# Activation sums of a seven-product MLP formed in the preceding output blocks, with changed waits and loads around them

## What is computed

```python
def sq_relu_mlp(h, w1, w2):
    u = jax.nn.relu(h @ w1)
    return (u * u) @ w2

x = x + mix                                             # mix = o @ w_out
x = x + sq_relu_mlp(rms_norm(x, norm_mlp[i]), mlp_w1[i], mlp_w2[i])   # 1024 -> 4096 -> 1024
```

## Time and profile before

| | us |
|---|---|
| median of 3 runs | 2312.28 (2311.3 to 2315.58) |
| the profiled execution | 2314.29 |
| its span, first to last instruction | 2312.3 |
| TensorE busy | 2238.0 (97%) |
| VectorE busy | 1347.2 (58%) |
| ScalarE busy | 891.5 (39%) |
| GpSimd busy | 319.6 (14%) |
| mean granted TensorE clock | 0.990 of full |

### The profile page before, as it was taken

The page is one execution under the profiler, slowest core; times in us unless marked ns, Lnnn a source line. Parts: engine busy times, 40 slices in busy tenths (PEclk is TensorE's granted clock), DMA queues, the critical chain, the costliest instruction groups (busy, mean ns, idle before and its releaser), DMA issues.

```text
span 2312.3 us, 30630 instructions
## 1 busy us (share of the span) xinstructions
PE 2238.0 (97%) x12667; PEld 1864.3 (81%) x12667; DVE 1347.2 (58%) x1560; ACT 891.5 (39%) x1188; POOL 319.6 (14%) x191
## 2 busy tenths in 40 slices
PE   9999999999999999999999799999999999799999
PEld 7888888878888888887966689889867767698998
DVE  6434445696543454584476656556568845654754
ACT  4212324354323223442276334244344664432532
POOL 1000001020101000120012203213102203031230
PEclk9999999999999999999999899999999999899999
DMA  5323223210323322223310233333234102234333
GB/s 185 98 90 104 91 77 115 74 60 30 109 91 103 97 91 86 98 89 113 92 51 19 64 119 101 109 119 101 69 104 110 37 19 82 73 91 137 101 91 109
DMA packets 201186, 208.12 MB, mean 90 GB/s; under 512 B 7042, under 2 KB 195218, under 8 KB 201076
## 3 DMA queue, kind: packets, MB, share of 16 engines
q1 hardware_dynamic: 201076, 206.56, 28.8%
HBM read 199.27 MB, written 2.10 MB: 87 GB/s over the span
## 4 chain that ended last, share of the span: by engine, by line
PE 82%; DVE 11%; ACT 3%; DMA 2%; issue 1%; POOL 1%; SPq 0%; ACTq 0%; DVEq 0%; POOLq 0%
PE psum L833 76%; DVE w_lo L340 3%; PE psum L921 2%; PE psum L923 2%; PE psum L922 2%; DMA w_raw<-in_mlp_w 2%; DVE w_lo L391 1%; DVE rstd L2246 1%; DVE sm L2830 1%; DVE xg_lo L2228 1%; POOL arena L3100 1%; ACT w_hi L378 1%; ACT w_hi L334 1%; DVE sx_raw L2231 0%; DVE sx_raw L2228 0%
## 5 line engine op out<-in xcount | busy, mean ns | idle before, releaser
L833 PE MATMUL psum<-xg_hi,w_hi 128*128 128x512 f32 (+1 forms) x1528 | 599.0, 392 | 20.7 <-DVE buf_a L2228 9.1
L833 PE MATMUL psum<-xg_lo,w_hi 128*128 128x512 f32 (+1 forms) x1576 | 610.2, 390 | 0.3 <-ACT free_x L1647 0.3
L833 PE MATMUL psum<-xg_hi,w_lo 128*128 128x512 f32 (+1 forms) x1528 | 594.7, 389 | 0.0
L378 ACT ACTIVATE w_hi<-w_raw 128x2048 fp32r<-128x2048 f32 x150 | 285.3, 1902 | 423.7 <-PE psum L833 375.5
L391 DVE TENSOR_TENSOR w_lo<-w_raw,w_hi 128x2048 fp32r<-128x2048 f32 x148 | 346.3, 2340 | 164.5 <-ACT w_hi L378 161.2
L833 PEld LDWEIGHTS psum<-xg_hi,w_hi 128*128 128x128 f32 x1528 | 287.9, 188 | 86.5 <-issue 11.4
L833 PEld LDWEIGHTS psum<-xg_lo,w_hi 128*128 128x128 f32 x1576 | 296.8, 189 | 62.8 <-ACT free_x L1647 1.4
L833 PEld LDWEIGHTS psum<-xg_hi,w_lo 128*128 128x128 f32 x1528 | 288.0, 188 | 60.0
L833 PE MATMUL psum<-h_hi,w_hi 128*128 128x512 f32 x696 | 277.3, 398 | 0.3 <-DVE h_lo L2228 0.3
L833 PE MATMUL psum<-h_hi,w_lo 128*128 128x512 f32 x696 | 271.4, 390 | 0.0
L833 PE MATMUL psum<-h_lo,w_hi 128*128 128x512 f32 x696 | 271.2, 390 | 0.0
(11 more groups left out here) (340 smaller groups left out, 3480.6 us busy)
## 6 DMA issues: line engine op xcount, KB each, us to landing
w_raw<-in_mlp_w SPq DMA_DIRECT2D x36, 1024.0 KB, 5.5
w_raw<-in_ffn_w_gate SPq DMA_DIRECT2D x21, 1024.0 KB, 5.3
w_raw<-in_ffn_w_up SPq DMA_DIRECT2D x21, 1024.0 KB, 5.3
w_raw<-in_mlp_w SPq DMA_DIRECT2D x42, 512.0 KB, 5.0
w_raw<-in_ffn_w_down SPq DMA_DIRECT2D x16, 1024.0 KB, 5.2
w_raw<-in_diff_w_in SPq DMA_DIRECT2D x12, 1024.0 KB, 5.1
w_raw<-in_w_in SPq DMA_DIRECT2D x9, 1024.0 KB, 5.1
w_raw<-in_dsa_w_in SPq DMA_DIRECT2D x9, 1024.0 KB, 5.5
```

The source lines that it names most:

```text
L378: e.activation(w_hi[:, wside(c), 0:n], w_raw[:, c % 2, 0:n], ACT.Copy).then_inc(sem("hi_done"), 1)
L833: return pe.matmul(out, lhsT, rhs, start=start, stop=stop)
```

## The change

- The four steps of the activation sums move from `square_pair` to the four output blocks before the stage, behind the split of the weights there, on ScalarE (`wout`) and VectorE (`residual`). `x_raw` lies in `buf_a` and `buf_c` by turns, so the second `w_run` is free of it, and a wait of SyncE for the sums goes.
- Product 0 of the first pair waits for `rms` alone, product 1 for the evacuation of the first up block and the sums.
- W22 goes into the half of `w_raw` that `raw22` names. In a one-pair group that is the other side than before, in a two-pair group the same.
- The first down block's load in mlp0 and mlp1 waits for the `w_lo` of strip 1 of the last pair in place of strip 5. It needs no other mark.
- Where the block waits for product 5 (one-pair groups), `hi` splits its first half after product 4. VectorE takes its `w_lo` there before the last evacuation steps instead of behind them.

```diff
-        x_raw = w_run[1].rearrange("p (a t) -> p a t", t=S)
...
+        def raw22_side(c0, q):
+
+            return (len(fast_groups[c0]) - q) % 2
+
+        def raw22(c0, q):
+
+            return raw(c0 + raw22_side(c0, q), 1)
...
             if isinstance(j, int) and c in freed_by:
-                e.wait_ge(*strip_mark("pe", *freed_by[c]))
+                first, n = freed_by[c]
+                if n % 7 == 5:
+                    e.wait_ge(*strip_mark("pe", first, n - 1))
+                    e.activation(w_hi[:, wside(c), 0:Q], w_raw[:, c % 2, 0:Q], ACT.Copy)
+                    e.wait_ge(*strip_mark("pe", first, n))
+                    e.activation(w_hi[:, wside(c), Q:used(c)], w_raw[:, c % 2, Q:used(c)], ACT.Copy).then_inc(sem("hi_done"), 1)
+                    return
+                e.wait_ge(*strip_mark("pe", first, n))
...
+        def x_raw(i):
+
+            return (buf_a, buf_c)[i % 2]
...
                     if q > 1:
                         sp.wait_ge(*strip_mark("lo", c0, 7 * (q - 2) + 6))
-                    if run_half[pair]:
-                        sp.wait_ge(*x_sums_ready(p, 3))
                     half(w_run[run_half[pair]], w2, 0, sem("w21_in"))
                     if q < 2:
-                        sp.wait_ge(sem("lo_done"), c0 - 1 + q)
+                        sp.wait_ge(sem("lo_done"), c0 - 1 + raw22_side(c0, q))
                     if q:
                         sp.wait_ge(*strip_mark("lo", c0, 7 * (q - 1) + 2))
-                    half(raw(c + q % 2, 1), w2, 1, sem("w22_in"))
+                    half(raw22(c0, q), w2, 1, sem("w22_in"))
...
-                    with sp.Fori(0, 2) as j:
-                        for s in range(2):
-                            load(sp, c + s, j, vd[:, :, bass.ds(j * 2 * BC + s * BC, BC)], nk=tiles)
+                    if name in FAST:
+                        c0 = c - 2 * (tiles // 4 - (g == 0))
+                        sp.wait_ge(*strip_mark("lo", c0, 7 * len(fast_groups[c0]) - 6))
+                        sp.dma_start(w_raw[:, c % 2, 0:tiles * BC].rearrange("p (k f) -> p k f", f=BC),
+                                     vd[:, :, 0:BC]).then_inc(sem(f"landed{c % 2}"), 16)
+                        for i in range(1, 4):
+                            load(sp, c + i, 0, vd[:, :, i * BC:(i + 1) * BC], nk=tiles)
...
-                    pe.wait_ge(sem("evac"), c0 - 1 if q == 0 else c0 + 2 * q - 2)
+                    if q:
+                        pe.wait_ge(sem("evac"), c0 + 2 * q - 2)
+                    else:
+                        pe.wait_ge(sem("rms"), p + 1)
                     product(0)
                     if q == 0:
+                        pe.wait_ge(sem("evac"), c0 - 1)
                         pe.wait_ge(*x_sums_ready(p, 3))
                     product(1)
...
                     def square_pair():
                         hi(act, c + 2)
-                        for i in range(2):
-                            x_split(p, i)
                         for s_ in range(2):
                             act.wait_ge(sem("hmul"), h0 + s_ + 1)
                             a(hidden(p)[0][:, 2 * s_:2 * s_ + 2, :], buf_d[:], ACT.Copy).then_inc(sem("h_hi_done"), 1)
-                            if s_ == 0:
-                                for i in range(2, 4):
-                                    x_split(p, i)
-                            else:
-                                hi(act, c + 3)
+                        hi(act, c + 3)
...
                     if name not in ("wout1", "wout2") or i:
                         hi(act, c + 2 + i)
+                    if p in (5, 7):
+                        x_split(p, i)
...
                     tt(buf_a[:, :, 0:TS], by_halves(side_sum), by_halves(buf_d[:, q % 2, :]), ALU.add).then_inc(sem("evac"), 1)
+                    if q == len(made) - 1 and len(made) % 2:
+                        lo(dve, after)
...
                 last_quarter(q)
-                if len(made) % 2:
-                    lo(dve, after)
...
                 if not split_first:
                     lo(dve, c + 2 + i)
+                if p_next in (5, 7):
+                    x_split(p_next, i)
+                    x_low(p_next, i)
```

More of the change, by code:

```diff
@@ L269, in turned_back @@
             return sem(f"rope_back{r % 2}"), 32 * (r // 2 + 1)
-        STEP = 1
         GROUPS = {"ffn1": GROUPS1, "ffn2": GROUPS1, "mlp0": GROUPS2, "mlp1": GROUPS2}
@@ L319, in strip_source @@
             if i == 5:
-                return raw(c + n // 7 % 2, 1), (sem("w22_in"), 16 * (pair + 1))
+                return raw22(c0, n // 7), (sem("w22_in"), 16 * (pair + 1))
             if i == 4:
-                return w_third, (sem("w_third"), STEP * (pair + 1))
-            return w_run[run_half[pair]], ((sem("w_first"), STEP * (pair + 1)) if i == 1 else
-                                     (sem("w_next"), STEP * (2 * pair + (1 if i == 2 else 2))))
+                return w_third, (sem("w_third"), pair + 1)
+            return w_run[run_half[pair]], ((sem("w_first"), (pair + 1)) if i == 1 else
+                                     (sem("w_next"), (2 * pair + (1 if i == 2 else 2))))
         def strip_hi(e, c0, n):
@@ L578, in fast_turn @@
         def fast_turn(p):
-            return FAST.index({0: "ffn1", 3: "ffn2", 5: "mlp0", 7: "mlp1"}[p])
+            return [5, 7].index(p)
         def x_sums_ready(p, i):
             return sem("x_sums"), 5 * (4 * fast_turn(p) + i + 1)
+        def x_raw(i):
+            return (buf_a, buf_c)[i % 2]
         def by_halves(v):
@@ L691, in ffn @@
                     vd = rows(wd, f0, tiles)
-                    with sp.Fori(0, 2) as j:
-                        for s in range(2):
-                            load(sp, c + s, j, vd[:, :, bass.ds(j * 2 * BC + s * BC, BC)], nk=tiles)
+                    if name in FAST:
[6 more added lines that the diff above has]
+                    else:
+                        with sp.Fori(0, 2) as j:
+                            for s in range(2):
+                                load(sp, c + s, j, vd[:, :, bass.ds(j * 2 * BC + s * BC, BC)], nk=tiles)
                     f0 += tiles
@@ L1667, in x_split @@
                 n = 4 * fast_turn(p) + i
-                if i:
-                    act.wait_ge(sem("x_sums"), 5 * n - 1)
                 for m in range(2):
-                    a(x_raw[:, m, :], x_res[:, 2 * i + m, :], ACT.Copy,
+                    a(x_raw(i)[:, m, :], x_res[:, 2 * i + m, :], ACT.Copy,
                       scale=ngain(p, 2 * i + m)).then_inc(sem("x_scaled"), 1)
@@ L2268, in x_split @@
                 dve.wait_ge(sem("x_scaled"), 3 * n + 2)
-                even, odd, z = x_raw[:, 0, :], x_raw[:, 1, :], sx_raw[:, :, i, :]
+                even, odd, z = x_raw(i)[:, 0, :], x_raw(i)[:, 1, :], sx_raw[:, :, i, :]
                 e1, e2, o1, o2 = even[:, 0:TS], even[:, TS:S], odd[:, 0:TS], odd[:, TS:S]
@@ L2381, in square_pair @@
                         lo(dve, c + 2)
-                        for i in range(2):
-                            x_split(p, i)
-                            x_low(p, i)
                         for s_ in range(2):
@@ L2391, in square_pair @@
                                ALU.subtract).then_inc(sem("h_done"), 1)
[L2392 to L2397, removed]
+                        lo(dve, c + 3)
                     if gated:
@@ L3118, in fast_sums @@
                         pool.wait_ge(*strip_mark("lo", c0, 7 * q + 1))
-                        add_rows(w_run[run_half[pair]], raw(c + q % 2, 1), sem("w_next"))
+                        add_rows(w_run[run_half[pair]], raw22(c0, q), sem("w_next"))
                         pool.wait_ge(sem("w21_third_in"), 16 * (pair + 1))
-                        add_rows(w_third, raw(c + q % 2, 1), sem("w_third"))
+                        add_rows(w_third, raw22(c0, q), sem("w_third"))
                         if q + 1 < len(made):
```

## The result

| | before | changed |
|---|---|---|
| median, us | 2312.84 (2311.3 to 2315.58, 4 runs) | 2275.11 (2273.54 to 2275.52, 4 runs) |
| ratio to before | | 0.9834, 95% interval 0.9817 to 0.9851 |
| profiled span, us | 2312.3 | 2273.7 |
| mean granted clock | 0.990 | 0.995 |

37.7 us were gained; 39.2 had been forecast, with 2273 for the median.

A forecast was written before the change was run, and what follows sets the result against it. TensorE is busy nearly all the time, so only its waits or low clock can go. 12.9 + 9.5 - 3.4 + 5.0 + 3.4 + 10.3 + 1.5 = 39.2 us off 2312.3 gives 2273 us, range 2261 to 2286.

The forecast's parts named there:

- The output blocks: Four blocks before each MLP stage: with a sums step each needs 11.67 us on VectorE, 0.8 more than TensorE.
- The chain to product 2: VectorE's path from fourth residual to product 2, first group: product 2 earlier by 9.5 us in mlp0, 12.9 in mlp1.
- Both holds by GpSimd: GpSimd sums delay VectorE 2.2 us each, before the fourth sums step and in the first up block's evacuation.
- Rival A: GpSimd holds nobody on the path to product 2: 8.8 us less, 2264; chance 0.17.
- One of the signs: Sign of a wrong forecast: product 2 starting later than 33 us after the fourth residual, a missed hold.
- Product 0: First group: starting right behind block 104 or 152, waiting for the sqrt alone, is worth nothing taken alone.
- The clock after the wait: Low clock on products 2 to 6 after the left-over wait: 1.7 us a stage, 3.4 us lost.
- Rival B: Clock or output blocks take more: left-over wait costs 6.2 us a stage, not 1.7; 2282; chance 0.15.
- The first down block: One-pair groups: wait 0.6 us instead of 3.17; 5.0 us gained, plus 3.4 of low clock.
- the group changes: Six changes from two-pair groups to down blocks: TensorE no longer waits, 10.3 us gained, plus 1.5 of low clock.
- C: Sums in output blocks bring nothing, product 2 starts as before: 20.2 us gained, 2292; chance 0.06.
- D: TensorE stays at 1.2 GHz from product 2 through four down blocks of each first group: 2360; chance 0.05.

The follow-up runs named there:

- the late first sum: Changed kernel, with GpSimd's first weight sum in one-pair groups waiting for the last activation sums: 2269.7 us, ratio 0.9810.
- the idle matmuls: Changed kernel plus 28 matmuls into an unread bank between products 1 and 2 of each one-pair group: 2271.0 us, ratio 0.9818.
- the load back: Changed kernel, with only the first down block's load waiting again for lo_done of the block before it: 2284.8 us, ratio 0.9872.
- the w_lo back: Changed kernel, with VectorE's w_lo of the first down block in one-pair groups again behind the last evacuation steps: 2281.0 us, ratio 0.9858.
- the run with the sums back: Changed kernel, with only the eight activation-sum steps returned to the first group (`square_pair`): 2295.3 us, ratio 0.9921.
- splitting the strips early: Changed kernel, with strips 2 and 3 of one-pair groups split before the second up block's evacuation: 2278.5 us, ratio 0.9851.
- the twelve traces: Profiles of the kernel before, the changed kernel and the ten experiments on the changed kernel.
- the run of idle matmuls with the late first sum: Changed kernel plus the 28 idle matmuls and GpSimd's first sum after the activation sums: 2270.9 us, ratio 0.9818.

## Why the prediction was right, step by step

**The output blocks.** 11.67 us between residuals had been forecast; they are 1282.96 - 1271.39 = 11.57 apart. The fourth residual slipped to 33.5 us after the first, 6.3 more than before (6.6 forecast). TensorE waited 2.0 us before the third output block and 0.35 before block 103, as expected. The w_lo of the output blocks took 2.3 us again, so the 4 us more that the prediction worked out for the case that GpSimd's sums of squares hold them did not come.

**The chain to product 2.** Forecast 9.5 us in mlp0 and 12.9 in mlp1, measured 10.1 and 13.4. Both holds by GpSimd are there: the pair of sums of 2.94 us is the first, and the late first sum showed that it is one. The second is split in two, the square of 2.39 us and the rest of 2.22 us where each takes 1.2: 2.2 us in sum. That second one was not tested by itself. Rival A, that nobody is held, gave 2264 and fell with these rows. One of the signs was set wrong: "product 2 starting later than 33 us after the fourth residual" was to speak against the prediction, whose own chain needs 33.7 us there in mlp1. Measured are 32.6 in mlp0 and 33.4 in mlp1, both within 0.4 of the chain.

**Product 0.** Worth nothing by itself, forecast and measured (2275.0 with its wait back).

**The clock after the wait.** This term was too small: 1.7 us a stage in the forecast, 2.4 and 2.0 measured, and the idle matmuls confirm the cause. Rival B had 6.2, which was far too much: the clock was back 5.7 and 4.5 us after product 2 started.

**The first down block.** Forecast 0.6 us of wait, measured 0.8. ScalarE's rows for the two halves and, below them, for the first down block of the second group:

```profile
1338.34 1.06 ACT L383 ACTIVATE w_hi<-w_raw 128x1024 fp32r<-128x1024 f32 x1 [4.22 <-PE psum L946]
...
1341.11 1.06 ACT L385 ACTIVATE w_hi<-w_raw 128x1024 fp32r<-128x1024 f32 x1 [1.71 <-PE psum L946]
...
1422.79 1.92 ACT L391 ACTIVATE w_hi<-w_raw 128x2048 fp32r<-128x2048 f32 x1 [3.27 <-PE psum L946]
```

The halves are ended by products 4 and 5, the whole block's split by product 11: none by a transfer. For the group changes the forecast was that no wait stays, and none did; with the load back 9.7 us were lost, and with the w_lo back 5.9. W22's new place and the two halves of w_hi were not taken back by themselves, so their share is not shown. The account for both kinds of place is 7.8 + 8.8 = 16.6 us after the down blocks began, against 10.3 + 1.5 + 3.4 = 15.2 forecast. The 1.4 us between them may be an overlap: without a wait a matmul of 0.28 us starts 0.12 us behind the one before, so a wait that goes is worth some 0.16 us more than its row says, 1 us for six. That is argued, not tested.

**The sum.** Forecast 39.2, by the two traces 38.6, by the medians 37.7. Rivals C and D did not show. C gave 20.2 us for a change whose sums bring nothing, and the run with the sums back had 18.6, so its price was about right, but in the changed kernel the sums are ready long before product 1, and the clock is at 1.00 in all down blocks of mlp0's first group. That the sum came so near is partly luck: small errors offset each other (1.1 us too little on the chain, 1.0 too little on the clock's cost, 1.4 too little behind the start of the down blocks, 0.3 too much at the first down blocks). Counted from the first residual the change gave 40.4, and the 1.9 us by which the changed trace came late to it, where single executions vary, bring that to 38.5.

## What to carry to other kernels

Work taken off a stage's critical engine may go beside a matmul-bound stage even if it doesn't fit there fully: here 3.8 us a block were moved where 3.0 were free, and the 0.8 us that were passed on cost little. Before moving a step forward, list everything that the waiting instruction needs, and move all of it: splitting the strips early did nothing as long as a copy of 0.6 us stayed behind, and with that copy and a part of strip 4 moved too it was 9 us faster (2273.3 to 2263.95, both with the late first sum). Look what GpSimd runs beside VectorE's instructions with two SBUF inputs; one added wait on GpSimd, off the path, brought 5 us.

## What the runs showed of the hardware

I had not expected that the clock would behave differently behind waits of the same length. Behind 3.17 us it was 0.71 in mlp0 of the kernel before; with the w_lo back it was 1.00 in mlp0 and 0.54 over 6 us in mlp1. Behind the 1.8 us with the load back it was 0.57, and behind a wait of 2.7 us in the kernel before (the second group change of mlp0) it was 1.00.

The clearest case is the wait of 2.0 us before the third output block, which ten of the twelve traces have, to within 0.02 us, and which the edits of these ten leave alone. The 4 us behind it, in the changed kernel and in the run of idle matmuls with the late first sum:

```profile
1279.28:1283.28 4.00, 4.00 (x17) 3.30 (x18) 2.84 (x6) 1.06 (x1) 0.00 (x0) 1.00 0.71 210
```

```profile
1279.45:1283.45 4.00, 4.00 (x11) 3.12 (x12) 2.84 (x6) 1.06 (x1) 0.00 (x0) 0.59 0.73 218
```

The clock fell there in six of the ten traces and stayed at 1.00 in four. So the length of a wait alone does not tell whether the clock falls, and a low stretch that one trace shows need not stand in another execution. Behind waits of 1.8 to 3.2 us a low stretch lost 1.5 to 2.8 us where it stood, and behind the waits of 7.3 to 7.6 us, 2.0 and 2.4 us after product 2 had started.
